# A seven-product down projection: the order of its products and of VectorE's work, its operand forms loaded in pieces, and a tail by halves of the tokens

## What is computed

```python
x = x + mixer(rmsnorm(x), ...)
x = x + (silu(xn @ w_gate) * (xn @ w_up)) @ w_down      # xn = rmsnorm(x)
y = rmsnorm(x) * final_g
```

## Time and profile before

| | us |
|---|---|
| median of 3 runs | 2338.83 (2338.46 to 2341.11) |
| the profiled execution | 2336.13 |
| its span, first to last instruction | 2334.4 |
| mean share of the full TensorE clock | 0.981 |
| weight loads of TensorE busy (PEld) | 2223.3 |
| VectorE busy | 1624.8 |
| ScalarE busy | 945.2 |
| POOL busy | 10.3 |

### The profile page before, as it was taken

The page is one execution under the profiler, slowest core; times in us unless marked ns, Lnnn a source line. Parts: engine busy times, 40 slices in busy tenths (PEclk is TensorE's granted clock), DMA queues, the critical chain, the costliest instruction groups (busy, mean ns, idle before and its releaser), DMA issues.

```text
span 2334.4 us, 41229 instructions
## 1 busy us (share of the span) xinstructions
PE 2237.9 (96%) x17550; PEld 2223.3 (95%) x17550; DVE 1624.8 (70%) x1910; ACT 945.2 (40%) x1229; POOL 10.3 (0%) x16
## 2 busy tenths in 40 slices
PE   9999999999999999999999999999998699999886
PEld 9999999999999999999999999999998699999875
DVE  6257444565444488888888888888885577777776
ACT  5334222123333354444444444444443334444453
POOL 0000000000000000000000000000000000000000
PEclk9999999999999999999999999999998899999997
DMA  5221342452233323544444435444359453553421
GB/s 186 91 73 68 107 146 97 145 185 91 91 110 110 111 88 125 167 142 132 157 132 159 149 124 165 141 133 159 130 164 365 162 216 125 198 199 98 175 82 77
DMA packets 119892, 325.40 MB, mean 139 GB/s; under 512 B 10491, under 2 KB 51515, under 8 KB 118748
## 3 DMA queue, kind: packets, MB, share of 16 engines
q1 hardware_dynamic: 119244, 323.69, 40.5%
q10 hardware_dynamic: 528, 0.07, 0.0%
HBM read 267.09 MB, written 56.63 MB: 139 GB/s over the span
## 4 chain that ended last, share of the span: by engine, by line
PE 85%; DVE 8%; DMA 3%; ACT 2%; issue 2%; POOL 0%; SPq 0%; POOLq 0%; DVEq 0%; ACTq 0%
PE acc L1043 30%; PE acc L837 30%; PE g L1043 21%; DMA w_raw<-w_d 3%; DVE w_lo L1535 2%; DVE w_s L1556 1%; DVE trunk L1576 1%; DVE w_raw L1556 1%; DVE trunk L1578 1%; DVE trunk L1589 1%; ACT w_hi L752 1%; ACT hst L722 0%; ACT tmp L700 0%; ACT trunk L776 0%; DMA h_dram<-hst 0%
## 5 line engine op out<-in xcount | busy, mean ns | idle before, releaser
L837 PE MATMUL acc<-op_hi,w_hi 128*128 128x272 f32 x1920 | 401.2, 290 | 1.3 <-DVE w_lo L1144 1.3
L837 PE MATMUL acc<-op_hi,w_lo 128*128 128x272 f32 x1920 | 397.7, 289 | 0.0
L837 PE MATMUL acc<-op_lo,w_hi 128*128 128x272 f32 x1920 | 396.3, 288 | 0.0
L1043 PE MATMUL acc<-sg_hi,w_hi 128*128 128x272 f32 x1056 | 313.0, 296 | 59.3 <-DVE trunk L1589 53.2
L1043 PE MATMUL acc<-op_hi,w_hi 128*128 128x272 f32 x1056 | 306.8, 291 | 8.4 <-ACT hst L722 6.5
L1043 PE MATMUL g<-op_hi,w_hi 128*128 128x272 f32 x1056 | 306.8, 291 | 3.1 <-issue 3.1
L1043 PE MATMUL acc<-sg_hi,w_lo 128*128 128x272 f32 x1056 | 309.4, 293 | 0.0
L1043 PE MATMUL acc<-sg_lo,w_hi 128*128 128x272 f32 x1056 | 308.0, 292 | 0.0
L837 PEld LDWEIGHTS acc<-op_hi,w_hi 128*128 128x128 f32 x1920 | 302.6, 188 | 4.0 <-issue 3.1
L1043 PE MATMUL g<-op_hi,w_lo 128*128 128x272 f32 x1056 | 306.3, 290 | 0.0
L1043 PE MATMUL acc<-op_hi,w_lo 128*128 128x272 f32 x1056 | 306.3, 290 | 0.0
(11 more groups left out here) (252 smaller groups left out, 4223.3 us busy)
## 6 DMA issues: line engine op xcount, KB each, us to landing
w_raw<-w_in SPq DMA_DIRECT2D x88, 512.0 KB, 3.3
w_raw<-w_gu SPq DMA_DIRECT2D x88, 512.0 KB, 3.2
w<-w_gu SPq DMA_DIRECT2D x88, 512.0 KB, 3.2
hf_dram<-hf_hi SPq DMA_DIRECT2D x22, 952.0 KB, 6.4
hf_dram<-hf_lo SPq DMA_DIRECT2D x22, 952.0 KB, 8.7
w_raw<-w_out SPq DMA_DIRECT2D x32, 512.0 KB, 3.2
w_raw<-w_d SPq DMA_DIRECT2D x32, 512.0 KB, 3.3
w<-w_d SPq DMA_DIRECT2D x32, 512.0 KB, 3.3
```

The source lines that it names most:

```text
L837: last = nc.tensor.matmul(acc[t % 2][:, a, 0:TH], w, x[:, k, a * TH:(a + 1) * TH], start=start and n == 0, stop=stop and n == 2)
L1043: last = nc.tensor.matmul(out, w, x, start=fresh and j == 0 and i == 0, stop=j == h - 1 and i == 2, skip_group_check=True)
```

## The change

In both stages the products are reordered so that C11 is complete after product 3, C22 after 4, C12 after 5 and C21 after 6. Products 0 and 1 alone start fresh; ScalarE now also copies pb into pd (`seed_d`), onto which product 6 accumulates, in place of the copy to `u3_sb`. `c_read` counts four reads per step. VectorE's order becomes: C11 of the step before, block_lo 0, C22, sum 0, C12, block_lo 1, two sums, C21, block_lo 2. Product 3's weights are w_12, those of 5 `w_s`, those of 6 w_22. `gate` and `up` move into `hst`, next to each other, and half of them is scaled by one operation; silu moves from idx 4 to idx 3.

```diff
-PAIRS_H = (4, 4, 4, 4, 3, 3)
+PAIRS_H = (3, 3, 4, 4, 4, 4)
-            banks = (pa, pc, pb, pd, pb, pa, pc)
+            banks = (pa, pc, pb, pa, pb, pc, pd)
-                fresh = idx in (0, 1, 3)
+                fresh = idx < 2
@@ load_block
-                elif j == 1:
-                    sp.wait_ge(s_made, 4 * s - 1)
+                elif j % 2:
+                    sp.wait_ge(s_made, 4 * s - 1 + j // 2)
                 else:
-                    sp.wait_ge(lo_ready, split(NP * (s - 1) + (4, 0, 3, 5)[j]))
+                    sp.wait_ge(lo_ready, split(NP * (s - 1) + 4 + j))
@@ SP, from gate/up to down
-            for s in range(1, FT + 1):
-                for j in (1, 2, 0, 3):
+            for s in range(1, FT):
+                for j in (1, 3, 0, 2):
                     load_block(s, j)
                 if s % 2 == 0 and s >= 4:
                     spill_hidden(s // 2 - 2)
+            spill_hidden(FT // 2 - 2)
             last = NP * (FT - 1)
             sp.wait_ge(hf_out, 32 * PAIRS_H[0])
-            for p in range(5):
+            for p, j in enumerate((1, 3, 0, None, 2, None, None)):
+                if j is not None:
+                    load_block(FT, j)
                 sp.wait_ge(chunk_done, done(last + p))
                 load_form(0, p)
...
-            for s in range(FT + 2, NS):
-                for j in (1, 2, 0, 3):
+            for s in range(FT + 1, NS):
+                for j in (1, 3, 0, 2):
                     load_block(s, j)
                 c, b = divmod(s - FT, BATCHES)
-                if b == 1 and 1 <= c < NCH - 1:
-                    for p in range(NP):
-                        sp.wait_ge(chunk_done, done(NP * (FT + BATCHES * c) - NP + p))
+                if c == 0 and b == 1:
+                    load_h(1)
+                    spill_hidden(FT // 2 - 1)
+                if c == 0 and b == 2:
+                    sp.wait_ge(hf_out, 32 * (FT // 2))
+                if c == 0 and b >= 2:
+                    load_h(b)
+                if b and c < NCH - 1:
+                    for p in ((0, 1, 2), (3, 4), (5, 6))[b - 1]:
+                        if c:
+                            sp.wait_ge(chunk_done, done(NP * (FT + BATCHES * c) - NP + p))
                         load_form(c + 1, p)
@@ ScalarE, block_hi
                 if idx == 1 and s >= 1:
-                    up_free(s - 1)
-                    to_sbuf(u3_sb, pb, s - 1, u3_out)
+                    seed_d(s - 1)
@@ VectorE, a down step's outputs
+                elif piece == C22:
+                    dve.wait_ge(u2_out, s + 1)
+                    dve.wait_ge(p5_out, s + 1)
+                    chain(nc.vector.tensor_tensor(y[:, :, :, 1, :], y[:, :, :, 1, :], up_sb, ALU.add))
+                    dve.wait_ge(seeded_d, s + 1)
+                    nc.vector.tensor_tensor(y[:, :, 1, 1, :], y[:, :, 1, 1, :], pb[:, :, 0:TH], ALU.add)\
+                        .then_inc(c_read, 1)
@@ VectorE, before step 0's forms
+                    if c + 4 == C_ST + 3:
+                        sum_block(0, 3)
...
-                dve.nop().then_inc(c_read, 6)
+                dve.nop().then_inc(c_read, 8)
@@ VectorE, the loop over steps
-                    if 1 <= idx <= 3:
-                        outputs(s - 1, idx)
                     if idx == 0:
+                        outputs(s - 1, C11)
+                    if idx == 1:
+                        outputs(s - 1, C12)
+                    if idx == 2:
+                        outputs(s - 1, C21)
+                    block_lo(s, idx)
+                    if idx == 0:
+                        if s >= 3 and s % 2 and s <= FT + 1:
+                            hidden_t_lo(s - 2)
+                        outputs(s - 1, C22)
                         sum_block(s, 0)
@@ VectorE, the tail
+            outputs(NS - 1, C11)
+            add_square(2 * KT - 5)
+            outputs(NS - 1, C22)
+            add_part(0)
+            add_part(1)
+            outputs(NS - 1, C12)
+            add_part(2)
+            dve.nop().then_inc(part_add, 4)
+            outputs(NS - 1, C21)
...
+            diagonal(1, 1)
+            dve.wait_ge(factor_psum, 1)
+            dve.wait_ge(y_scaled, 12)
+            scale(1, pb, range(0, 4, 2))
+            diagonal(0, 2)
+            scale(1, pb, range(4, NV_OUT, 2))
+            dve.wait_ge(factor_psum, 3)
+            scale(0, pc, range(0, NV_OUT, 2))
```

More of the change, by code:

```diff
@@ L62 @@
 NS = FT + NCH * BATCHES
-HID_FORM = (0, 3, 6, 5, 4, 1, 2)
+HID_FORM = (0, 3, 6, 1, 4, 2, 5)
+TAIL = NS - BATCHES
+C11, C22, C12, C21 = range(4)
+PARTS = ((0, 0), (1, 1), (0, 1), (1, 0))
+T_AT = (1, 2, 4, 6)
 MIX_ORDER = list(range(HK, KT)) + list(range(HK))
@@ L276, in build @@
         h_out = sem("h_out")
-        h_in = sem("h_in")
+        h_in = [sem(f"h_in{i}") for i in range(BATCHES)]
         xg_done = sem("xg_done")
@@ L331, in split, with rows @@
             return C_ST + n - 1
+        def rows(b):
+            return trunk[:, 4 * b:4 * b + 4, :].rearrange("p (q r) (t c) -> p q r t c", r=2, t=2)
         def pairs_of(s):
@@ L1105, in _ @@
                     product(C_ST + NP * s + idx, NP * s + idx, (0, 1), PAIRS_H[ch], 4 * (ch % 2))
-            pe.wait_ge(hsq_add, 2 * KT + 1)
-            for n, buf in enumerate((rstd[:], tmp[:, (KT - 1) % 2, :])):
-                if n == 1:
-                    pe.wait_ge(hsq_done, 2 * KT)
-                for j, (at, _, _) in enumerate(BLOCKS):
-                    last = nc.tensor.matmul(g01[:, n, j:j + 1], buf[:, at:at + P], onesf[:, 0:1], start=True, stop=True)
-            last.then_inc(var_done, 1)
@@ new lines, in factor @@
+            def factor(a, bank, side):
+                for j in range(3):
+                    at, skip, w = BLOCKS[j]
+                    last = nc.tensor.matmul(bank[:, side, at + skip:at + skip + w], onesf[:],
+                                            diag[:, (3 * a + j) * P + skip:(3 * a + j) * P + skip + w],
+                                            start=True, stop=True, skip_group_check=True)
+                last.then_inc(factor_psum, 1)
+            pe.wait_ge(c_read, 4 * NS + 4 + C12 + 1)
@@ L1125, in _ @@
+            pe.wait_ge(part_add, 4)
+            column_sums(1, (rstd[:, TH:T],))
+            column_sums(0, (rstd[:, 0:TH], sq4[3][:, 0, :], sq4[3][:, 1, :]))
+            pe.wait_ge(diagonals, 1)
+            factor(1, pb, 0)
+            factor(1, pb, 1)
+            pe.wait_ge(diagonals, 2)
+            factor(0, pc, 0)
+            factor(0, pc, 1)
         @block.vector
@@ L1531, in block_lo @@
                 n = NP * s + idx
-                src = (w_11, w_s[:], w_s[:], w_22[:], w_11, w_12[:], w_s[:])[idx]
+                src = (w_11, w_s[:], w_s[:], w_12[:], w_11, w_s[:], w_22[:])[idx]
                 w, slot = columns(s), (C_ST + n) % RING
@@ L1586, in outputs @@
+                dve.wait_ge(chunk_done, done(n + (3, 4, 5, 6)[piece]))
+                if s < FT:
+                    if piece == C11:
+                        if s == 0:
+                            dve.wait_ge(h_out, 16 * HK)
+                            dve.wait_ge(std_done, 1)
+                            chain(nc.vector.reciprocal(rstd[:], rstd[:]))
+                        else:
+                            dve.wait_ge(hid_done, s)
                         nc.vector.tensor_tensor(gate[:, 0:TH], pa[:, q, 0:TH], rstd[:, 0:TH], ALU.mult)\
@@ L1600, in outputs @@
                             .then_inc(gate_in, 1)
                     else:
-                        nc.vector.tensor_tensor(rows(b)[:, :, 0, 1, :], rows(b)[:, :, 0, 1, :], pc[:, :, 0:TH], ALU.add)\
+                        nc.vector.tensor_tensor(up[:, 0:TH], pd[:, q, 0:TH], rstd[:, 0:TH], ALU.mult)\
                             .then_inc(c_read, 1)
-                        dve.wait_ge(c_read, 6 + 3 * s + 3)
-                        last = nc.vector.tensor_tensor(rows(b)[:, :, :, 1, :], rows(b)[:, :, :, 1, :], up_sb, ALU.add)
```

325 lines of the change are left out of this document (157 added, 168 removed).

## The result

The changed kernel takes **2264.66 us** (median of 4 runs, 2262.02 to 2265.70) against 2339.97 (2338.46 to 2346.56) of the kernel before in the same comparison: ratio 0.967, 95% interval 0.965 to 0.969. Forecast: 2253, range 2244 to 2276. The time lies in the range, and no rival came true at its price. But 15 of the 85.8 us did not come; the steps that failed are named in the part on why the prediction was right or wrong.

The account below looks back on a forecast made before the run. TensorE was busy throughout gate/up; down lost 82.1 us to waits for VectorE, loads and ScalarE, with 29.8 behind its last matmul. Savings of 45.3 + 33.4 - 1.3 + 8.4 = 85.8 us gave 2253, range 2244 to 2276.

Parts of the forecast that it names:

- Order of products: Down from its fourth step: TensorE's wait for VectorE to add pa in every step goes, 45.3 us saved.
- 8.32 us with three pairs ... due at 9p, 9.08 us later: 0.8 us to spare: Down step: chain making the next weights, from 5p to block 2's split; p is one product's time, counted from step start.
- Rival E: Down: the step's wait only moves, block 2 being as late as C11 was; costs the 45 us, 2298; chance 0.08.
- The last batches: End of down: ScalarE finishes one row after each of four products, 4.8 us per step; its waits go, within the 45.3.
- Loads: First three down steps: smaller, spread loads leave 3.5 us of waits in place of 36.9, 33.4 us saved.
- up to 1 us: Second and third down steps: VectorE's work late by this much for products 1 and 2, w_11 landing behind the spill.
- Rival B: Beginning of down: loads in one ordered queue still hold it, one stall of 20 us, 2273; chance 0.19.
- Gate/up: Steady gate/up steps: w_22, loaded later, lands at 15.9 to 16.0 us, wanted at 16.0; no change on 44 steps.
- rival C: Gate/up: w_22 comes too late and holds VectorE; 163 us at a landing time of 11 us, 2416; chance 0.03.
- Start of gate/up: One more operation of 1.22 us ahead of c_read's release, and one added matmul of 0.1: 1.3 us lost.
- Tail: After the last matmul: end at 21.4 us instead of 29.8, 8.4 us saved; stores at 410 GB/s.
- Rival D: Tail: the halved stores of 272 KB do not overlap, some 25 us more than forecast, 2278; chance 0.04.

Follow-up runs that it names:

- w21_in_place: Changed kernel with w_11 - w_21 written over w_21 instead of w_11, and the two blocks' places in the load queue exchanged: 2255.37 us.
- order_only: Kernel before with only VectorE's order changed in down: pa is added ahead of block_lo(s, 1) and the two sums: 2325.05 us, ratio 0.994.
- forms_later: Changed kernel with the second chunk's first three forms loaded after the third down step's blocks, not the second's, the others one step later too: 2261.81 us.
- seed_first: Changed kernel with ScalarE, in the third down step, copying pb to pd ahead of w_11's cast, and the Sqrt table loaded one step earlier: 2262.34 us.
- w21_forms_sum: Changed kernel with w_11 - w_21 written over w_21, second set of forms loaded later, and sum_block(0, 3) back behind c_read's release: 2250.16 us, ratio 0.962.
- factor_in_sbuf: Changed kernel with VectorE scaling half 0 in the tail by the factor copied to SBUF instead of the one in PSUM: 2262.59 us.

## Why the prediction was right or wrong

**Order of products: right, but its chain was taken to start on time.** The forecast was 45.3 us, 40.2 came. The step that failed reads "8.32 us with three pairs ... due at 9p, 9.08 us later: 0.8 us to spare". The sum itself holds: in w21_in_place 0.7 us were to spare. But it lets VectorE add C22 at 5p, and left out how the chain comes to its start: the reload of w_11 after the split for product 4, 4.17 us, its cast, and its split, which stands ahead of C22 on VectorE. In after C22 began 1.24 to 1.46 us late, more than the 0.8. With the load the chain closes on itself at 16.7 us, and each step of the second chunk lasts that; w21_in_place took the load out, and all 5.1 us came. Rival E named the place ("block 2 is late") and over-priced it: there were six waits of 0.5 to 0.9 us in five steps, not as much as C11's in every one. The other fifteen four-pair steps last 21.2 us as forecast, and order_only shows that VectorE's order alone does not do it.

**The last batches: right.** They were counted into the 45.3. After's last four steps take 84.75 us, four times 21.19. Spreading `finish` gives 5.0 us there and 1.8 in the tail; the short chunks moved to the front give 6.6 and 5.0, and pay about 5 for it in the loop.

**Loads: the mechanism right, the term mis-sized: 8.9 us lost where I took 3.5.** I had seen that w_11 of the third step lands late, and priced it by VectorE's lag, "up to 1 us". It landed some 8.6 us after its issue and ScalarE stood 7.2 us for it: this is the term that was mis-sized, and forms_later, which changes the queue's order alone, gets 6.2 us back. I also did not ask what stands behind the waiting cast on ScalarE, `seed_d`, for a product of the step that is running; seed_first shows that this sets only the place of the wait. The two small waits of the second step (0.95 and 0.88) came as predicted, those of the third did not. w_d's blocks land in 4.2 and 3.3 us by the median (forecast: under 10); the four of the third step took 7.1 to 9.4. Rival B, one stall of 20 us, did not occur; its mechanism did, at a quarter of the price.

**Gate/up: right.** Loads of w_gu land in 3.6 and 3.2 us. TensorE waits twice in its first two steps (0.6 and 0.8 us) and not at all in the steady ones, and rival C had nothing behind it.

**Start of gate/up: 2.9 lost for 1.3.** The failed step is "sum_block(0, 3) is moved ahead of the release of c_read ... one more operation of 1.22 us": the sum stands there in the code, but the wait for `c_read` grew by only 0.4 us, and TensorE had its release before the sum began. It is the forms of the last row, behind the sum on VectorE, that came late: product 1 starts 9.13 us after product 0 (before: 8.49), and its 24 matmuls take 5.6 us in place of 4.5, since all of them start 227 ns apart (granted clock 0.50, after TensorE had stood 3.7 us) where in before the last ten were back at 126. w21_forms_sum took 1.6 us of it back.

**Tail: 21.6 for 21.4, by luck: two errors cancel.** The last scaling ends 13.5 us after the last matmul, not 15.9: six column sums took 1.47 us where I reckoned with 0.43 each. They began 0.9 us after down's last matmul and ran at a granted clock of 1.00 (2243.2 to 2246.3 us); in before TensorE had stood 6.0 us, and the clock there was 0.50 (2310.7 to 2316.0). The stores ate that: I took 410 GB/s and measured 356. Diagonal 0, which I costed at nothing against a rule, lasted 0.56 us as it does alone; there POOL paid, 2.79 for 2.63. By the Trainium skill, *SBUF — State Buffer*, "SBUF: two separate sides", whichever of the two begins first holds the port for its whole instruction and the other one waits; the traces agree (in factor_in_sbuf VectorE 1.41 us where POOL began first, in after POOL 2.79 where VectorE did). The rule was right, and the price small because of who came first.

**Rival D** did not come true: sixteen stores of 272 KB overlap, landing in 3.5 us at 356 GB/s together.

## What to carry to other kernels

When a chain between engines seems to have time to spare, follow it round once, from the event back to itself in the step before, through buffers and loads too: what counts is its length against the step, not the slack behind a point at which everything is assumed to be there. Where a load is late, list what stands behind the waiting instruction on its engine, for the step that runs as well as for the next. And to read one output sooner was worth little here (6.9 us) while the order of the products finished two of them at the step's end.

## What was not expected of the hardware

In factor_in_sbuf VectorE's operations with both inputs in SBUF and POOL's took turns by whole instructions: 6.17 and 3.64 us for what takes 3.87 and 2.63 when VectorE's factor is in PSUM. Stores of 272 KB in rows of 1088 bytes ran at 356 GB/s, of 544 KB in rows of 4352 at 411. And in the same code, at 63.5 us, with TensorE busy and at the full clock throughout the 9 us before, the granted clock was 1.00 for the next 6.9 us in the profile of before and 0.63 in that of after; in both, eight matmuls on 33 rows had begun at 62.2 us. What makes the difference was not tried and stays open.
